# Four more modulation blocks on VectorE, and a gate projection cut in two halves, in a two-network transformer kernel

## The reference

```python
def first_block(x, p, ...):
    for i in range(2):
        h = rmsnorm(x, norm_mix_g[i])
        if i % 2 == 0:
            ... # y_a: 8 heads of a decaying recurrence; y_b: 4 heads of a gated delta rule
            y_b = gdn_group(proj[..., o_bq:o_bg], proj[..., o_bg:o_bb], ...)   # the second one is the gate
            mix = jnp.concatenate([y_a, y_b], -1) @ even_w_out[e]
        else:
            mix = chunk_band_attention(...) @ attn_w_out[o]
        x = x + mix
        hf = rmsnorm(x, norm_ffn_g[i])
        x = x + jnp.square(jax.nn.relu(hf @ mlp_w1[i])) @ mlp_w2[i]            # 1024 -> 4096 -> 1024
        x = x + rmsnorm(p[i] @ ple_w_proj[i], ple_norm_g[i]) * jax.nn.sigmoid(x @ ple_w_gate[i])
    return x

def gdn_group(qkv, gate, ...):
    ...
    o = chunk_gated_delta_rule(q, k, v, beta, g)       # chunks of 64, a triangular solve in each
    o = rmsnorm(o, norm_g) * jax.nn.silu(heads(gate))

def second_block(x, c, ctx, c_ctx, w_ada, b_ada, ...):
    for layer in range(2):
        mod_l = (jax.nn.silu(c) @ w_ada[layer] + b_ada[layer])[:, None, :]     # 1024 -> 6144
        mod_c = jax.nn.silu(c_ctx) @ w_ada[layer] + b_ada[layer]
        sh1_l, sc1_l, g1_l, sh2_l, sc2_l, g2_l = jnp.split(mod_l, 6, axis=-1)
        ... # mixer and feed-forward, shifted and scaled by sh, 1 + sc, and gated by g
    return x_l
```

## Time and profile before

| | |
|---|---|
| Time, median of 3 | 1992.21 us (1992.2 to 1994.08) |
| The profiled execution | 1992.95 us, span 1990.8 us, mean granted PE clock 0.994 |
| PE busy | 1950.6 us, 98% of the span |
| DVE busy | 1202.2 us, 60% |
| ACT busy | 390.6 us, 20% |
| POOL busy | 34.3 us, 2% |
| DMA | 296.90 MB, mean 149 GB/s |
| Loads of columns | 36 of 512 KB, median 4.9 us from issue to landing |
| Loads of weight blocks | 111 of 2 MB, median 7.9 us |

### The profile page before, as it was taken

One profiled execution on the slowest core, in us unless ns is written; L12 is line 12 of the kernel. 1 busy time (PEld: TensorE's weight loads), 2 busy tenths in 40 slices (PEclk: granted clock), 3 DMA queues, 4 the chain that ended last, 5 costly groups with the idle time before them and its releaser, 6 DMA issues.

```text
span 1990.8 us, 26223 instructions
## 1 busy us (share of the span) xinstructions
PE 1950.6 (98%) x11422; PEld 1383.7 (70%) x11422; DVE 1202.2 (60%) x1705; ACT 390.6 (20%) x805; POOL 34.3 (2%) x65
## 2 busy tenths in 40 slices
PE   8999999999999999999999999999999999999998
PEld 7786669844675896448844648888874466669973
DVE  4555748785557687725445825555565574836776
ACT  2323020001214100031114712111100212321110
POOL 0000000000000000000000000000000000000000
PEclk8999999999999999999999999999999999999999
DMA  6435855654443556442241012222225443124442
GB/s 243 186 146 204 342 203 191 222 226 171 187 170 124 206 212 232 173 148 108 85 169 43 1 42 85 85 85 85 85 89 202 173 171 148 43 85 170 170 162 92
DMA packets 27490, 296.90 MB, mean 149 GB/s; under 512 B 3232, under 2 KB 3648, under 8 KB 10480
## 3 DMA queue, kind: packets, MB, share of 16 engines
q1 hardware_dynamic: 19728, 261.83, 34.9%
q0 software_dynamic: 7648, 33.40, 4.7%
HBM read 294.13 MB, written 1.08 MB: 148 GB/s over the span
## 4 chain that ended last, share of the span: by engine, by line
PE 90%; DVE 8%; ACT 1%; issue 1%; DMA 0%; SPq 0%; DVEq 0%; ACTq 0%
PE bank L358 88%; PE bank L721 1%; DVE small L890 1%; DVE arena L911 1%; PE bank L814 0%; DMA X<-in_x 0%; DVE arena L732 0%; DVE arena L517 0%; DVE arena L904 0%; DVE arena L675 0%; DVE arena L885 0%; DVE arena L1139 0%; ACT arena L848 0%; DVE arena L631 0%; DVE HT L2583 0%
## 5 line engine op out<-in xcount | busy, mean ns | idle before, releaser
L358 PE MATMUL bank<-arena 64*64 64x64 f32 (+8 forms) x4548 | 629.6, 318 | 13.2 <-DVE arena L517 2.4
L358 PEld LDWEIGHTS bank<-arena 128*128 128x128 f32 (+3 forms) x4548 | 433.2, 167 | 190.9 <-issue 149.6
L358 PE MATMUL bank<-HT,ring 128*128 128x128 f32 (+1 forms) x2400 | 396.1, 324 | 3.7 <-ACT arena L652 2.1
L358 PEld LDWEIGHTS bank<-HT,ring 128*128 128x128 f32 x2400 | 351.9, 191 | 43.0 <-issue 9.5
L358 PE MATMUL bank<-ring,arena 128*128 128x512 f32 (+1 forms) x674 | 295.6, 593 | 0.0
L358 PEld LDWEIGHTS bank<-ring,arena 128*128 128x128 f32 (+1 forms) x674 | 126.7, 190 | 154.7 <-issue 154.3
L358 PE MATMUL bank<-ring,HT 128*128 128x512 f32 (+1 forms) x480 | 189.4, 552 | 1.0 <-ACT HT L2069 0.8
L358 PE MATMUL bank<-arena,ring 128*128 128x128 f32 (+4 forms) x1158 | 187.2, 322 | 1.1 <-issue 1.1
L358 PEld LDWEIGHTS bank<-arena,ring 128*128 128x128 f32 (+3 forms) x1158 | 165.4, 189 | 16.2 <-issue 3.1
L358 PEld LDWEIGHTS bank<-ring,HT 128*128 128x128 f32 x480 | 85.4, 190 | 97.8 <-issue 94.6
L358 PE MATMUL bank<-HT,arena 128*128 128x128 f32 (+2 forms) x800 | 126.7, 322 | 0.0
(11 more groups left out here) (322 smaller groups left out, 1568.9 us busy)
## 6 DMA issues: line engine op xcount, KB each, us to landing
ring<-in_W SPq DMA_DIRECT2D x111, 2048.0 KB, 7.9
arena<-in_adaT POOLq DMA_DIRECT2D x36, 512.0 KB, 4.9
arena<-in_W SPq DMA_DIRECT2D x5, 2048.0 KB, 11.7
ring<-in_W SPq DMA_DIRECT2D x6, 1536.0 KB, 8.7
ring<-in_W SPq DMA_DIRECT2D x4, 1024.0 KB, 9.2
arena<-in_rel POOLq DMA_DIRECT2D x1, 2048.0 KB, 11.2
arena<-in_rpb POOLq DMA_DIRECT2D x1, 2048.0 KB, 9.5
arena<-gate_rows POOLq DMA_DIRECT2D x1, 2048.0 KB, 15.5
```

What stands on the lines that cost most here:

```text
L358: return nc.tensor.matmul(out_, lhsT, rhs, start=start, stop=stop, skip_group_check=True)
```

## The change

- PE now computes 11 modulation blocks (ada1.0 to ada1.7 and ada0.9 to ada0.11); ada1.8 to ada1.11 become 16 more columns on DVE (52 in all), and `adaT` grows by them.
- The 16 columns stand as follows: one more in each of the eight up pairs of the two feed-forwards, between the joins "z" and "w"; one more in chunk 0 of down0, between the right sums and the other two columns; two more in each of the chunks 0, 1, 2 of down1, between the right sums and the left sums (four each now); and a seventh at the end of the attention.
- The bias and the scales of layer 1 go with the columns. The turning of layer 1's gate rows, two matmuls and what follows, moves from eout to the end of mlp1, and ACT's work on the context tokens waits for column 51 instead of 35.
- `pe_bgate(1)` is cut into two halves of four matmuls: the first stands at the end of step 2 of the gdn inversion, the second in step 4. Its bank is held in between, ACT's silu of it follows step 4, and its weight slot is barred for the modulation blocks in between.
- `pe_ada` calls stand elsewhere: none ahead of the rwkv inversion; in it, one in step 4, one in step 5 and one at its end (four before); in gdn four (seven before).

Core of the diff:

```diff
-ADA = [f"ada1.{j}" for j in range(12)] + [f"ada0.{j}" for j in range(9, 12)]
+ADA = [f"ada1.{j}" for j in range(8)] + [f"ada0.{j}" for j in range(9, 12)]
...
+        if names[i] in ADA[1:9]:
+            allowed.remove(slots[names.index("bgate")][0])
...
-        def pe_bgate(t):
+        def pe_bgate(t, ks=range(KT)):
...
-            ps = open_bank(f"gate b.{t}")
-            for k in range(KT):
+            if ks[0] == 0:
+                open_bank(f"gate b.{t}")
+                state["held"].add(banks[f"gate b.{t}"])
+            ps = PS[banks[f"gate b.{t}"]]
+            for k in ks:
...
-            pe_ada(1)
             pe_half_block("bqkv0", "bq", 0, 0)
...
                 elif k == 4:
-                    pe_bgate(1)
+                    pe_ada(1)
                     pe_bnorm_sum()
                 else:
-                    pe_ada(3)
+                    pe_ada(2)
                     pe_bnorm_spread()
...
-                elif k == 4:
-                    pe_ada(2)
-            pe_ada(4)
+            pe_ada(3)
...
+                elif k == 4:
+                    pe_bgate(1, range(4, KT))
                 else:
-                    pe_ada(k + 5)
+                    pe_ada(6)
                 if k == 3:
-                    pe_ada(7)
+                    pe_ada(5)
                 pe_xlx("gdn", k, 0, LX2, XT2)
                 if k < 4:
                     pe_chunk_out(k)
-                    pe_ada((5, 6, 8)[k - 1])
-            pe_ada(11)
+                if k == 1:
+                    pe_ada(4)
+                elif k == 2:
+                    pe_bgate(1, range(4))
+            pe_ada(7)
...
                 dve_seven_c(l, 0, "z", a[:, :, P:SEQ], UM1, k4)
                 if p < 3:
                     dve_row_sums(f"up{i}.{p + 1}", 0, up_pair(i, p + 1), slice(0, 512), US, (5, 7), prev=l)
+                dve_columns(1)
                 dve_seven_c(l, 0, "w", b[:, :, 0:P], UM1, k4)
...
                 dve_right_sums(f"down{i}", n, names, kt, M["right"])
+                dve_columns(((1, 0, 0, 0), (2, 2, 2, 0))[i][n])
                 if 1 <= n < 3:
                     dve_left_sums(f"down{i}", n + 1, HH[:, 8 * n + 8:8 * n + 16, :], M["left"][(n + 1) % 2])
                 dve_columns(((2, 2, 2, 1), (2, 2, 2, 0))[i][n])
...
-            dve_columns(6)
+            dve_columns(7)
```

More of the change, by code:

```diff
@@ L315, in at @@
             return marks[name][1]
-        state = {"bank": 0, "last": [None] * 8, "w": 0, "held": None, "column": 0}
+        state = {"bank": 0, "last": [None] * 8, "w": 0, "held": set(), "column": 0}
         pe = Steps(nc.tensor, tensor_done, marks)
@@ L325, in open_bank @@
             if b is None:
-                if state["bank"] % 8 == state["held"]:
+                while state["bank"] % 8 in state["held"]:
                     state["bank"] += 1
@@ L329, in open_bank @@
                 state["bank"] += 1
-            assert b != state["held"]
+            assert b not in state["held"]
             if state["last"][b]:
@@ L1078, in pe_ada @@
                 open_bank("ada")
-                state["held"] = banks["ada"]
+                state["held"].add(banks["ada"])
             ps = PS[banks["ada"]]
@@ L1087, in pe_ada @@
                 pe.mark("ada")
-                state["held"] = None
+                state["held"].remove(banks["ada"])
         def dve_ada_rows():
@@ L1126, in act_wide, with column_of @@
             act.mark("c wide")
+        def column_of(j):
+            return 2 * j if j < 36 else 96 + 2 * (j - 4)
         def dve_columns(n):
@@ L1145, in dve_mod_columns @@
             tt(MOD[:, 0], MOD[:, 0], C("bada0", 0, 48).unsqueeze(2).broadcast_to([P, 48, 2]), ALU.add).then_inc(vector_done, dve.one())
+            tt(MOD[:, 1, 32:48], MOD[:, 1, 32:48], C("bada1", 32, 16).unsqueeze(2).broadcast_to([P, 16, 2]), ALU.add).then_inc(vector_done, dve.one())
             dve_scales(0)
+            dve_scales(1)
         def pe_lora_up():
@@ L1197, in pe_half_block @@
             pe.mark(name)
-        def pe_bgate(t):
+        def pe_bgate(t, ks=range(KT)):
             if t == 0:
-                state["block"] = weight("bgate").rearrange("p (k c) -> p k c", k=KT)
-            ps = open_bank(f"gate b.{t}")
-            for k in range(KT):
-                last = mm(ps[:, :], ht(k, t), state["block"][:, k, :], k == 0, k == KT - 1)
-            if t:
-                weight_used(last, "bgate")
-            else:
-                last.then_inc(tensor_done, pe.one())
-            pe.mark(f"gate b.{t}")
+                state["bgate"] = weight("bgate").rearrange("p (k c) -> p k c", k=KT)
+            if ks[0] == 0:
[3 more added lines that the diff above has]
+            for k in ks:
+                last = mm(ps[:, :], ht(k, t), state["bgate"][:, k, :], k == 0, k == KT - 1)
+            if ks[-1] == KT - 1:
+                if t == 0:
+                    state["held"].remove(banks["gate b.0"])
+                if t:
+                    weight_used(last, "bgate")
+                else:
+                    last.then_inc(tensor_done, pe.one())
+                pe.mark(f"gate b.{t}")
         ABW = flat(T1[:, 5])
@@ L1464, in pe_mix @@
                     pe_chunk_out(k)
-                    pe_ada((5, 6, 8)[k - 1])
-            pe_ada(11)
+                if k == 1:
+                    pe_ada(4)
+                elif k == 2:
+                    pe_bgate(1, range(4))
+            state["held"].remove(banks["gate b.1"])
+            pe_ada(7)
             pe.wait_ge(vector_done, at("gdn ready"))
@@ L1484, in pe_mix @@
                 if c < 3:
-                    pe_ada(12 + c)
+                    pe_ada(8 + c)
                 pe_bchunk_out(c)
@@ L1501, in act_bq, with act_gate_b @@
             act.mark(f"bq kept{j}")
+        def act_gate_b(t):
+            ps = full(act, f"gate b.{t}")
+            activation(GB[:, t, :], ps[:, :], ACT.Silu).then_inc(scalar_done, act.one())
+            act.mark(f"read gate b.{t}")
         def act_mix():
@@ L1577, in act_mix @@
                 if k == 4:
-                    for t in range(2):
-                        ps = full(act, f"gate b.{t}")
-                        activation(GB[:, t, :], ps[:, :], ACT.Silu).then_inc(scalar_done, act.one())
-                        act.mark(f"read gate b.{t}")
+                    act_gate_b(0)
                     act.wait_ge(vector_done, at("conv5"))
@@ L2197, in act_mlp @@
                 act_gate_rows(0)
+                act_gate_rows(1)
             act_turn_all(f"xt{i}", [0, 1])
@@ L3581, in put, with cols @@
         blocks[name] = tiled(w)
-    def cols(prefix, w, at=0, skip=0):
-        for i in range(skip, w.shape[1] // 512):
+    def cols(prefix, w, at=0, blocks=None):
+        for i in blocks or range(w.shape[1] // 512):
             put(f"{prefix}{at + i}", w[:, i * 512:(i + 1) * 512])
```

34 lines of the change are left out of this document (16 added, 18 removed).

## The result

| | before | after |
|---|---|---|
| Time, median | 1992.3 us (1992.2 to 1994.08) | 2017.79 us (2016.9 to 2021.8) |
| Ratio | | 1.0134, 95% interval 1.0121 to 1.0147 |
| Profiled execution, span | 1992.95, 1990.8 us | 2017.24, 2015.2 us |
| Mean granted PE clock | 0.994 | 0.990 |
| Loads of columns | 36 | 52 |

The change makes the kernel 1.3% slower; the forecast was 2014.7. From here on "shift" is the start of a PE row after less the start of the same row before, in the two profiled executions.

What follows compares the result with a forecast made beforehand. The prediction took PE, busy 98% of the span, to bound the kernel, with DVE having room on average. Terms of -6.3, 2 x 1.2, 2 x 1.4, 18.1, 1.8, 2.0 and 1.7 summed to +22.5: median 2014.7 us, range 2001 to 2021.

Steps and rivals of the forecast that it cites:

- mixer: Both inversions: PE loses calls but waits some 1.3 for DVE's reciprocal; -6.3 us, between -9 and -3.
- gate rows in eout, in mlp1: Layer 1's gate rows: two matmuls only move, 0; ACT's copies at the second feed-forward's end 0 to 1, taken as 0.
- up pairs, first and second: Up projections: 2.6 us more DVE work per column makes m4 wait; +1.2 a feed-forward, between 0.8 and 2.4.
- last column ahead of down, first and second: End of each up projection: last column waits for a load issued among weight loads; 0 to 4, taken as 1.4 each.
- down chunks of the second: Second feed-forward's down chunks 0 to 2: third column's load lands late behind two weight loads; 4.4, 4.4 and 9.3, sum +18.1.
- down chunk 0 of the first: First feed-forward's down projection: three columns where two stood, DVE's period 25.9 against PE's 24.1; +1.8 (0 to 2).
- attention: End of the attention: seventh column's load delays DVE's additions by 3.8 against 1.8 of slack; +2.0 (0.8 to 3.8).
- clock: Down projection: long PE waits bring one more drop to 1.2 GHz; +1.7 (0 to 7, one for each long wait).
- The main term: Down projections, chiefly the second's: DVE waits for the third column's load behind weights; +18.1, at the other end +26.
- Hidden everywhere: Rival: DVE's extra work costs nothing in the down projections and PE keeps the mixer's gain; 1986 to 1989 us, chance 0.07.
- Worse contention: Rival: every new column waits 11.2 us for its load and the clock falls each time; 2022 to 2028, chance 0.05.
- norm rows late: Rival: norm rows, loaded later, land after DVE needs them in the gdn branch; 2022 us, chance 0.03.

Runs made afterwards that it cites:

- The run without the load: Changed kernel, the seven new down-chunk columns not loaded; DVE does the same products on numbers already in the buffer: 1998.45 us, ratio 1.0044.
- the early loads: Changed kernel with some down-chunk columns put ahead of the last right sums, so their loads are issued ahead of the weights': 2009.77 us, ratio 1.0094.
- the better placement: Changed kernel, same 52 columns placed anew, three buffers in the down projections, one early column per chunk: 1984.11 us, ratio 0.9969; second time 1983.71, ratio 0.9961.
- the kernel with three buffers: Changed kernel, all columns in their places, the down projections loading them into three buffers in place of two: 2007.68 us, ratio 1.0087.

## Why the prediction held

By its own steps, in us of shift:

| step | predicted | measured |
|---|---|---|
| mixer | -6.3 | -6.27 |
| gate rows in eout, in mlp1 | 0 | -0.57, +0.22 |
| up pairs, first and second | +1.2, +1.2 | +1.40, +2.47 |
| last column ahead of down, first and second | +1.4, +1.4 | +2.56, +2.40 |
| down chunks of the second | +18.1 | +17.3 |
| down chunk 0 of the first | +1.8 | +1.8 |
| attention | +2.0 | +2.15 |
| clock | +1.7 | +2.6 |
| waits in the second network | 0 | -1.8 |
| sum | +22.5 | +24.4 (0.1 between the rows) |

- **The main term**, the second feed-forward's chunks, was right in mechanism, place and size. DVE's period was forecast as 28.5 and 30.3; it is 28.1 and 30.3. DVE's waits in the third column, 8.59, 5.89 and 4.11, are about the 5 to 9 forecast. PE's waits at m5, forecast as 4 or more, are 2.27, 3.83 and 2.47, since a slow group ahead or the transposes' own wait of 4.25 took the rest. The run without the load shows that it is the load, and the early loads of 3.7 to 4.0 show that it is slow because the weights are ahead of it.
- **The mixer** came out within 0.1, and part of that is luck. The wait for the reciprocal came as forecast (1.3, measured 1.35). But the -6.27 holds differences of executions that the change doesn't touch: in its first 32 us the profiled execution after gained 2.3, of which 1.35 by 64 matmuls that took 15.74 in place of 17.09, and near 100 us it lost 2.9, by an "issue" wait of 1.69 in place of 0.48 and a group of 8.86 in place of 7.17. Without the two the mixer's shift is about -6.8.
- **Down chunk 0 of the first feed-forward** has its +1.8, but two causes fit it. DVE's L519 comes 26.0 apart there (25.9 forecast), and PE's m5 group runs slow (15.67 in place of 13.97), which alone makes 25.8. The run without the load still has 25.5. So the agreement doesn't show that the load costs anything there.
- **The attention** lost 2.15, with PE's wait of 1.99.
- **The mis-sized terms** are the up pairs of the second feed-forward and the last column. For the last column I took 1.4 of a range of 0 to 4, and PE's wait grew by 2.5 and 2.4. Its load, issued when its buffer comes free, again is among weight loads: in the second it is issued at 766.0, within 1 us of a weight load, and lands 8.8 later. DVE waits 2.6 and 2.5 for it. For the up pairs I counted only DVE's 2.6 of work and took the first feed-forward's slack for both. In the second PE waits 1.83 at m4 of pair 1, where it waits 0.83 in the first. No column load is late there. DVE starts the row sums of a pair later, because it waits longer for a weight block, 1.79 in place of 1.02:

```profile
304.33 4.49 DVE L633 TENSOR_TENSOR arena<-ring 128x2048 f32<-128x2048 f32 x2 [1.02 <-DMA ring<-in_W]
...
687.43 4.49 DVE L633 TENSOR_TENSOR arena<-ring 128x2048 f32<-128x2048 f32 x2 [1.79 <-DMA ring<-in_W]
```

- **The clock**: the sum was near by compensation. There are four slow stretches in the m5 groups, and I had counted one. The first two of the second feed-forward cost nothing, since DVE set the pace behind them: the m5 group of chunk 0 takes 1.4 longer, and PE's wait ahead of the next is that much shorter. The one in the first feed-forward stands in that chunk's +1.8. The last, behind the 4.25 and 2.47, is paid for with 2.6. In the kernels where DVE no longer sets the pace, such a stretch costs its 1.4 to 2.8 in full. By the Trainium skill ("TensorE: Matmul & The Clock Gate", Part 1) idleness lets the clock fall to 1.2 GHz. The trace agrees that it falls behind such waits, with 0.91 and 0.58 granted. To price each fall at 1.7, as the prediction tried, would have been too dear, since DVE's pace hid two of the four.
- **The rivals.** "Hidden everywhere" named the right point: the third column's load. In the better placement, where that load has time, the gain of the mixer does come through. "Worse contention" and "norm rows late" didn't happen: in each chunk one product waited for its load, and not two. The two loads that the kernel after issued at 803.04 and 831.18, while DVE multiplied columns, landed in 3.9 and 3.8, no later than others away from the weights. The trap of the Trainium skill ("SBUF — State Buffer", SBUF: two separate sides), a load from GpSimd held up while VectorE holds the shared port, doesn't show here.

## What to carry to other kernels

A busy share of 60% says how much work an engine can take, and not where. A load that is issued by the use of a buffer belongs to the step: look at what else that same moment releases, since a small transfer queued behind two large ones costs their time. Moved work fits if its data are requested ahead of the large loads and its place is ahead of a wait that is there anyway; here the same 52 columns go with a kernel that is 25 us slower than before in one placement, and 6 to 8 faster in another with a third buffer.

## What the runs showed that I had not expected

The same kernel differs from one execution to the next by whole events. The better placement ran twice with a profile, with spans of 1986.9 and 1981.3. Near 100 us PE waits for something that the profile doesn't show ("issue"), 1.98 in the one and 0.37 in the other, and after the longer one the following matmuls take 8.86 in place of 7.17:

```profile
100.89 0.67 PE L379 MATMUL bank<-arena 64*64 64x64 f32 x26 [1.98 <-issue]
101.50 8.86 PE L379 MATMUL bank<-HT,ring 128*128 128x256 f32 x32
```

```profile
95.97 0.67 PE L379 MATMUL bank<-arena 64*64 64x64 f32 x26 [0.37 <-issue]
96.58 7.17 PE L379 MATMUL bank<-HT,ring 128*128 128x256 f32 x32
```

That makes 3.3 between the two, of 5.6 between the spans. Another 3.3 lies ahead of it, in the first 31 us, where the same 64 matmuls take 17.01 in the one and 14.05 in the other; about 1 us is made up later. A wait of a certain length doesn't always bring the slow stretch: in the kernel with three buffers the m5 group behind 3.89 took 13.97, while the ten other m5 groups behind waits of 3.5 to 3.9, one of them in the same kernel, took 15.4 to 16.7:

```profile
779.59 13.97 PE L379 MATMUL bank<-arena 128*128 128x512 f32 x32 [3.89 <-DVE arena L538]
```
